# Expert stage of a two-layer diffusion backbone: six fixed split buffers, wider up matmuls, another order of the loads at the start

## The reference, cut to what matters

```
h = x * (1 + sc) + sh;   x = layer_norm(alpha * x + gate * f(h))     # each of four sub-layers
sh, sc, gate, ... = split(silu(c) @ w_mod + b_mod)                   # the modulation
hc = ctx * (1 + csc1) + csh1;   k_c, v_c = hc @ w_kv                 # context keys and values, layer 0
# experts: rows of x sorted by expert
top_logit, top_e = top_k(h @ w_router, 2);  gates = softmax(top_logit)
for e in range(8):                                                   # D = 1024, hidden 3584
    y[rows of e] = (silu(h[rows] @ w1[e]) * (h[rows] @ w3[e])) @ w2[e]
out = sum over a token's two experts of gate * y
```

## Time and profile before

| | |
|---|---|
| median of 3 runs | 2552.37 us (2550.55 to 2554.25) |
| the profiled execution | 2551.86 us, span 2550.1 us |
| TensorE busy | 2309.6 us, 91% of the span |
| VectorE, ScalarE, GpSimd busy | 1509.1, 1115.8, 346.6 us |
| moved | 514.6 MB, 202 GB/s over the span |

### The profile page before, as it was taken

One profiled execution on the slowest core, in us unless ns is written; L12 is line 12 of the kernel. 1 busy time (PEld: TensorE's weight loads), 2 busy tenths in 40 slices (PEclk: granted clock), 3 DMA queues, 4 the chain that ended last, 5 costly groups with the idle time before them and its releaser, 6 DMA issues.

```text
span 2550.1 us, 38310 instructions
## 1 busy us (share of the span) xinstructions
PE 2309.6 (91%) x14692; PEld 2024.5 (79%) x14693; DVE 1509.1 (59%) x1340; ACT 1115.8 (44%) x1075; POOL 346.6 (14%) x211
## 2 busy tenths in 40 slices
PE   5999979999987996698999999999999999999990
PEld 4866757887875875588999999988888889998880
DVE  3456565434476445487444444468888884445886
ACT  3135432222223223476333433357777774334771
POOL 0000118888560000100000000000000000000004
PEclk7989989999998996799999999999999999999995
DMA  6420155554431211788544545468898885545873
GB/s 279 182 83 1 71 230 194 183 183 149 179 116 66 99 66 50 268 335 303 187 180 174 200 180 183 181 243 329 335 346 325 345 334 209 190 171 197 313 279 132
DMA packets 76452, 514.62 MB, mean 202 GB/s; under 512 B 8272, under 2 KB 8400, under 8 KB 19056
## 3 DMA queue, kind: packets, MB, share of 16 engines
q1 hardware_dynamic: 61632, 444.55, 46.7%
q0 software_dynamic: 14768, 69.35, 7.4%
HBM read 484.51 MB, written 29.36 MB: 202 GB/s over the span
## 4 chain that ended last, share of the span: by engine, by line
PE 82%; DVE 10%; issue 3%; ACT 2%; DMA 2%; POOL 0%; DVEq 0%; ACTq 0%; SPq 0%; POOLq 0%
PE ps L1427 25%; PE ps L1429 24%; PE ps L1428 24%; DVE lo L1001 3%; PE ps L540 2%; PE ps L495 2%; PE ps L551 2%; PE ps L1665 1%; DVE hl L1352 1%; DMA raw<-w_mod 1%; PE ps L499 1%; PE ps L1468 1%; DMA xg<-dispatched_x 0%; DVE xz L1097 0%; DVE rstd L1091 0%
## 5 line engine op out<-in xcount | busy, mean ns | idle before, releaser
L1001 DVE TENSOR_TENSOR lo<-raw,hi 128x2048 fp32r<-128x2048 f32 x397 | 928.4, 2357 | 214.4 <-ACT hi L767 212.1
L767 ACT ACTIVATE hi<-raw 128x2048 fp32r<-128x2048 f32 x397 | 760.0, 1914 | 507.2 <-PE ps L1429 497.9
L1427 PE MATMUL ps<-hi,xth 128*128 128x256 f32 x2464 | 706.1, 287 | 13.8 <-DVE xtl L1332 12.9
L1429 PE MATMUL ps<-hi,xtl 128*128 128x256 f32 x2464 | 700.0, 284 | 0.0
L1428 PE MATMUL ps<-lo,xth 128*128 128x256 f32 x2464 | 699.9, 284 | 0.0
L1427 PEld LDWEIGHTS ps<-hi,xth 128*128 128x128 f32 x2464 | 475.3, 193 | 25.3 <-DVE xtl L1332 14.3
L1428 PEld LDWEIGHTS ps<-lo,xth 128*128 128x128 f32 x2464 | 475.5, 193 | 1.9
L1429 PEld LDWEIGHTS ps<-hi,xtl 128*128 128x128 f32 x2464 | 475.3, 193 | 0.0
L1427 PE MATMUL ps<-ah,hi 128*128 128x512 f32 x688 | 272.4, 396 | 19.2 <-DVE al L1063 12.9
L1427 PE MATMUL ps<-hi,hh 128*128 128x512 f32 x616 | 248.8, 404 | 28.9 <-DVE hl L1352 28.9
L1428 PE MATMUL ps<-al,hi 128*128 128x512 f32 x688 | 270.7, 393 | 0.0
(11 more groups left out here) (230 smaller groups left out, 2490.7 us busy)
## 6 DMA issues: line engine op xcount, KB each, us to landing
raw<-w_moe SPq DMA_DIRECT2D x338, 1024.0 KB, 4.8
raw<-w_pre SPq DMA_DIRECT2D x59, 1024.0 KB, 4.8
raw<-w_mod POOLq DMA_DIRECT2D x28, 1024.0 KB, 5.1
raw<-w_mod SPq DMA_DIRECT2D x20, 1024.0 KB, 7.2
dispatched_x<-zt POOLq DMA_DIRECT2D x22, 512.0 KB, 15.0
xg<-dispatched_x POOLq DMA_DIRECT2D x8, 1024.0 KB, 5.8
expert_y<-ys POOLq DMA_DIRECT2D x8, 1024.0 KB, 5.6
expert_y<-zt POOLq DMA_DIRECT2D x6, 512.0 KB, 24.6
```

What stands on the lines that cost most here:

```text
L767: act.activation(HI[h][:], RAW[r][:], ACT.Copy).then_inc(hi_ready[h], 1)
L1001: dve.tensor_tensor(LO[h][:], RAW[r][:], HI[h][:].bitcast(F32), ALU.subtract).then_inc(raw_used[r], 1)
L1427: pe.matmul(outp, wh, ah, start=first, stop=False, skip_group_check=True)
L1429: return pe.matmul(outp, wl, ah, start=False, stop=last, skip_group_check=True)
```

## The change

In the expert stage: six pairs of split buffers in place of three. Units 0 and 1 lie side by side in one tile (`HIA`, `LOA`), 2 and 3 in another, so that one up matmul takes 2x256 columns, w1 and w3 of one half, into one bank per row tile. The order in an expert is staggered over the halves and groups; the down product of the second half runs in the next group, behind up of the first half. The next expert's rows are transposed in the last group, ahead of its last down product. ScalarE and VectorE no longer wait for TensorE at each position, but at the silu and at the transposed hidden tile, whose waits cover the buffers. The result is started by `start` flags and no longer zeroed. SP's queue waits for the first rows to land before it loads on. The overflow path is rewritten alike.

At the start: another order of the loads; the first split is made while modulation is still running; the small matmuls run between the units of w_mod; ScalarE makes the high parts of context and x from the source; TensorE takes the context tile by tile.

```diff
+        HIA = put("hia", [P, 2, KD, 256], F32R, o_hi)      # LOA at o_lo, HIB at o_ah, LOB at o_al
+        HI5 = put("hi5", [P, UNIT], F32R, r2 + 49152)
+        LO5 = put("lo5", [P, UNIT], F32R, r2 + 57344)
-        MOE_BODY = [(p, p % 3) for p in range(6)]
+        WHERE = {0: (0, 0), 1: (1, 1), 5: (2, 5), 2: (3, 3), 3: (4, 4), 4: (5, 2)}   # unit: raw, split
 SP, start
-            for u in range(MOD_A):
+            for u in range(6):
                 load(u % 4, w_mod[u])
-            sp.dma_start(MASKF[:], maskin[:, 1, :]).then_inc(mask_in, 16)
             sp.dma_start(CX[:], ctxT_in).then_inc(cxin, 16)
             load(0, w_pre[0])
+            for u in (6, 7):
+                load(u % 4, w_mod[u])
             sp.dma_start(XZ[:], xT_in).then_inc(xin, 16)
+            sp.dma_start(MASKF[:], maskin[:, 1, :]).then_inc(mask_in, 16)
 SP, experts
+            def next_units(at):
+                for j in (0, 1):
+                    load(WHERE[j][0], unit(at + (6 + j)))
+                load(WHERE[5][0], unit(at + 5))
+                for j in (2, 3, 4):
+                    load(WHERE[j][0], unit(at + (6 + j)))
+            first_units(0, (0, 1, 2))
+            sp.wait_ge(stats_in, 3)
+            first_units(0, (3, 4))
             sp.wait_ge(routed, 1)
-            sp.wait_ge(scattered, 16 * 8)
+            sp.wait_ge(xg_in, 16)
+            with t.loop(sp, NE * GROUPS - 1, RAW_TURN) as g:
+                next_units(g * 6)
 ScalarE, start
+            for p in range(3):
+                mod_row(p)
+            full_split(0, 0)
+            mod_row(3)
...
             for k in range(KD):
-                act.wait_ge(ctx_tmp, k + 1)
-                act.activation(CXH[:, k, :], TMP[k % 2][:, 0:CTX], ACT.Copy).then_inc(cxh_ready, 1)
+                act.activation(CXH[:, k, :], CX[:, k, :], ACT.Identity, bias=MOD[:, 1, k:k + 1],
+                               scale=CG[:, k:k + 1]).then_inc(cxh_ready, 1)
+            act.wait_ge(xin, 16)
             for k in range(KD):
-                to_hi(k)
+                act.activation(AH[:, k, :], XZ[:, k, :], ACT.Identity, bias=MOD[:, 0, k:k + 1],
+                               scale=COEF[:, 0, 0, k:k + 1]).then_inc(ah_ready, 1)
+            act.wait_ge(tmp_ready, KD)
             for k in range(KD):
                 act.activation(XZ[:, k, :], XZ[:, k, :], ACT.Copy, scale=ALPHA).then_inc(alpha_done, 1)
 ScalarE, experts
+            def silu(q):
+                act.wait_ge(up_done[q], t.n(("up", q)))
+                act.activation(SE[:], up_view(q, 0), ACT.Silu).then_inc(se_ready, 1)
+            def group(upto=None):
+                silu(0)
+                high(0)
+                hidden(0)
+                high(1)
+                high(5)
+                silu(1)
+                high(2)
+                hidden(1)
+                if upto is not None:
+                    for i in range(3):
+                        token_tiles(i)
+                high(3)
+                if upto is not None:
+                    token_tiles(3)
+                    result(upto)
+                high(4)
 VectorE, start
+            split(0, 0)                      # now ahead of the modulation's sums
-            for k in range(KD):
+            for k in range(KD + 1):          # TMP of tile k, then CXL of tile k - 1
 VectorE, experts: group()
+                gated(0)
+                low_part(4)
+                hidden(0)
+                low_part(0)
+                low_part(1)
+                gated(1)
+                low_part(5)
+                hidden(1)                    # last group: token_tiles(0..2)
+                low_part(2)                  # last group: token_tiles(3), result
+                low_part(3)
 TensorE, start
-            for u in range(MOD_A):
-                mod_unit(u % 4, PS[:, u // 2, (u % 2) * 256:(u % 2 + 1) * 256])
+            for p in range(MOD_A // 2 + 1):  # two units, then the four small matmuls of the pair before
...
-            pe.wait_ge(cxl_ready, KD)
-                            for c in range(2):
-                                for k in range(KD):
+                            for k in range(KD):
+                                pe.wait_ge(cxl_ready, k + 1)
+                                for c in range(2):
 TensorE, experts
+            def up(q, tiles, r=None):
+                for j in (2 * q, 2 * q + 1):
+                    arrived(j)
+                hi, lo = ((HIA, LOA), (HIB, LOB))[q]
+                for s in range(tiles):
+                    for i, k in enumerate(ks):
+                        ins = three(PS[:, 2 * q + s, :], XTH[:, k, cols_], XTL[:, k, cols_],
+                                    hi[:, :, k, :], lo[:, :, k, :], i == 0, i == KD - 1)
+                ins.then_inc(up_done[q], 1)
+            def expert(tiles, r, more):
+                up(0, tiles, r)
+                turn_hidden(0, tiles)
+                up(1, tiles)
+                pe.wait_ge(ys_a, r)
+                pe.wait_ge(ys_b, r)
+                down(0, tiles, True)
+                turn_hidden(1, tiles)
+                with t.loop(pe, GROUPS - 1, turn):
+                    up(0, tiles)
+                    down(1, tiles)
+                    turn_hidden(0, tiles)
+                    up(1, tiles)
+                    down(0, tiles)
+                    turn_hidden(1, tiles)
+                if more:
+                    pe.wait_ge(xg_in, r * 16 + 16)
+                    for i in range(3):
+                        token_tiles(i)
+                down(1, tiles).then_inc(y_full, 1)
+                if more:
+                    token_tiles(3)
```

More of the change, by code:

```diff
@@ L262, in program @@
         raw_used = [sem(f"raw_used{i}") for i in range(6)]
[L263 removed]
+        hi_ready = [sem(f"hi_ready{i}") for i in range(6)]
         unit_done = [sem(f"unit_done{i}") for i in range(3)]
@@ L626, in _ @@
             t.skip(("raw", 3), 1)
-            per_g = {("raw", r): 1 for r, _ in MOE_BODY}
             def unit(i):
                 return w_moe[bass.ds(i, 1), :, :].rearrange("o p n -> (o p) n") if not isinstance(i, int) else w_moe[i]
-            def group(first):
-                for j in range(2, 8):
-                    load(j % 6, unit(first + j))
-            for j in range(4):
-                load(j, unit(j))
-            sp.wait_ge(routed, 1)
-            sp.wait_ge(scattered, 16 * 8)
@@ L643, in _, with first_units @@
-            for j in range(4, 8):
-                load(j % 6, unit(j))
-            with t.loop(sp, GROUPS - 1, per_g, 1) as g:
-                group(g * 6)
-            with t.loop(sp, NE - 1, times(per_g, GROUPS), 1) as e:
-                with t.loop(sp, GROUPS, per_g) as g:
-                    group(e * (6 * GROUPS) + g * 6)
+            def first_units(at, units):
+                for j in units:
+                    load(WHERE[j][0], unit(at + j))
+            def next_units(at):
[4 more added lines that the diff above has]
+                    load(WHERE[j][0], unit(at + (6 + j)))
@@ L653, in _ @@
[L653 to L655 removed]
+                with t.loop(sp, n_over, times(RAW_TURN, GROUPS)) as x:
                     e = sp.value_load(RI[0:1, bass.ds(x + 8, 1)], min_val=0, max_val=NE - 1)
[L657 to L660 removed]
+                    first_units(e * (6 * GROUPS), (0, 1, 2, 3, 4))
+                    with t.loop(sp, GROUPS - 1, RAW_TURN) as g:
+                        next_units(e * (6 * GROUPS) + g * 6)
+                    load(WHERE[5][0], unit(e * (6 * GROUPS) + (6 * GROUPS - 1)))
@@ new lines, in last_group @@
+            def last_group(r):
+                silu(0)
+                hidden(0)
+                high(5)
+                silu(1)
+                hidden(1)
+                result(r)
+            turn = dict(RAW_TURN)
+            turn.update({("up", 0): 1, ("up", 1): 1, "ht": 2})
+            turn_e = times(turn, GROUPS)
+            turn_e["xt"] = 4
+            for j in (2, 3, 4):
+                high(j)
+            for i in range(4):
+                token_tiles(i)
+            with t.loop(act, NE - 1, turn_e) as e:
+                with t.loop(act, GROUPS - 1, turn):
+                    group()
+                group(e + 1)
@@ new lines, in last_group @@
+            def last_group(r):
+                gated(0)
+                low_part(4)
+                hidden(0)
+                gated(1)
+                low_part(5)
+                hidden(1)
+                result(r)
+            turn = {("hs", h): 1 for _, h in WHERE.values()}
+            turn.update({"se": 2, "hh": 2})
+            turn_e = times(turn, GROUPS)
+            turn_e["xth"] = 4
+            dve.sem_inc(ys_b, 1)
+            dve.wait_ge(scattered, 16 * 8)
+            low_part(2)
@@ new lines, in either @@
+            def either(e, r, more):
+                count = pe.value_load(RI[0:1, bass.ds(e, 1)], min_val=0, max_val=T)
+                saved = dict(t.at)
+                with pe.If(count < P + 1):
+                    expert(1, r, more)
```

(8 more changed lines are left out.)

372 lines of the change are left out of this document (170 added, 202 removed).

## The result

The changed kernel takes 2439.37 us (median of 4 runs, 2438.57 to 2440.11); the kernel before, run beside it, 2552.11 (4 runs, 2550.55 to 2554.25). The ratio is 0.9558, with a 95% interval of 0.9541 to 0.9574: 113 us faster. The forecast was 2454, 15 us above, inside the range. The profiled execution took 2438.57 us, 0.8 under the median (span 2436.7).

The account below looks back on a forecast made before the run. TensorE was taken as the bound, four fifths of the chain of waits, mostly one split matmul's three partial products. Terms 23 + 54 + 3.5 + 6.4 + 10.5 = 97.4; 2551.9 - 97.4 = 2454 us; 8-in-10 range 2434 to 2488.

Parts of the forecast that it names:

- two-tile groups: Groups of 512 hidden features in experts over 128 rows: wider up matmuls give 33.75 us, 1.11 less; 21 groups, 23 us.
- one-tile groups: Groups in experts whose rows fit one tile: TensorE alone sets 17.3 us against 18.83; 35 groups, 54 us gained.
- between experts: Row transposes, splits and hand-overs between the eight experts: 42.3 us falls to 38.8, 3.5 us gained.
- start of the experts: First load of an expert's rows no longer shares with weight loads: lands in 5.8 us, not 12.2; 6.4 us gained.
- start of the kernel: Earlier context and first-unit loads and splits: second weight unit ready at 58.7 us against 69.47, 10.5 us gained.
- (d): Up matmuls: widening is worth nothing, 512 columns cost 0.240 us; 2495 us; chance 0.04.
- The layout of the group: One-tile group: down covers silu and product, VectorE is never behind, every wait is covered; 17.3 us.
- (a): One-tile groups: DMA sets the pace, about 18 us a group; 24 less gained, 2478 us; chance 0.12.
- (b): One-tile groups: hand-overs decide, a split ahead of a small op stalls each half; 18.3 us, 2490 us; chance 0.12.
- (c): Up matmuls: the two-piece moving operand restarts the stream, 0.31 us apart; slower, about 2756 us; chance 0.03.
- the gap rule: Up matmuls: columns divided by the clock plus some 2.5 ns, so a merged pair saves only 2.5 ns; sum 2486.
- The 358 GB/s: One-tile groups' weight loads: HBM side binds a core near this rate; 17.6 us a group, sum 2464.

Follow-up runs that it names:

- narrow: The changed kernel with each up matmul of 512 columns cut back into two of 256; order, buffers and waits stay: 2483.14 us.
- less_pe: The changed kernel without the third partial product (high weights by the hidden tile's low part) of every down projection: 2323.29 us.
- less_pe_half: The changed kernel without the down projections' third partial product and without half the columns of each load of an expert's next weight unit: 2322.96 us.
- contig: The changed kernel with a half's two units interleaved in the split buffers, so the up matmuls' moving operand is one run of 512 columns: 2439.57 us.
- fill: The changed kernel with the transposes of an expert's first hidden half moved behind the first twelve matmuls of its second up half: 2430.69 us.
- no_cover: The changed kernel with the down product of the half before put ahead of up 0; buffers, width and other engines' order stay: 2606.98 us.
- start_only: The kernel before with only the edits of the start of the kernel, the experts untouched: 2542.69 us.
- fill_early: fill with the high part of the second weight unit made ahead of the scaling of x on ScalarE: 2430.47 us.
- fill_first: fill with, on VectorE in an expert's first group, the second half's product put ahead of the low part of next unit 1: 2440.3 us.

## Why the prediction was right, and where its sizes were off

The direction and the place of each gain were right. Within the span, before and after differ by 113.4 us, and the traces divide them so:

| step | forecast | measured | from |
|---|---|---|---|
| two-tile groups, 21 | 23 | 26.3 | 34.86 - 33.61 |
| one-tile groups, 35 | 54 | 68.6 | 18.83 - 16.87 |
| between experts | 3.5 | 3.0 | rest 42.3, now 1335.6 - 1296.3 = 39.3 |
| start of the experts | 6.4 | 6.9 | rows' issue to first up, 15.5 and 8.6 |
| start of the kernel | 10.5 | 10.7 | first scatter 1027.97 and 1017.28 |
| end of the kernel | 0 | -2.0 | last store to end, 59.3 and 61.3 |

**The mis-sized term is the one-tile group: 17.3 forecast, 16.87 measured, 14.6 us over 35 groups, nearly all that the forecast was high; the other differences add up to 1.5.** Two things were wrong in "72x0.229 + 0.84". First the pace: the eleven intervals of the earlier trace rows that gave 0.229 begin with the first matmuls of a run, which are the slow ones. In after the matmuls of 512 columns stand 0.2267 us apart, up and down alike, read from the starts of two runs of down matmuls: 1693.98 to 1696.47 is 11 intervals of 0.2266, 1702.41 to 1704.00 is 7 of 0.2267. That makes 72 x 0.0023 = 0.17 us a group. The two starts of the first run in after:

```profile
1693.98 0.39 PE L1509 MATMUL ps<-hi,hh 128*128 128x512 f32 x1
...
1696.47 0.39 PE L1511 MATMUL ps<-hi,hl 128*128 128x512 f32 x1
```

Second, the 0.84 that I took over as "transposes and restarts" was the remainder behind one named stall. In after the remainder is 16.87 - 72 x 0.2267 = 0.55, so 0.29 of it was something else. The trace of before has it: a second wait for VectorE, once in a one-tile group, behind the transposes. The transposes and the next weight load in before:

```profile
1743.12 0.38 PE L1665 MATMUL ps<-small,he 128*128 128x128 f32 x2
...
1743.52 0.19 PEld L1427 LDWEIGHTS ps<-hi,xth 128*128 128x128 f32 x1 [0.26 <-DVE lo L1001]
```

And its waits in 1700 to 1837 us, the seven groups of one expert:

```profile
PEld ps L1427 <- DVE lo L1001: 1.8, 7, 0.3
```

From these transposes to the next matmul 0.40 us pass in 33 of the 35 one-tile groups; behind the group's other transposes it is 0.13, and in after and narrow it is 0.13 behind both, an expert's first and last group aside. So 0.27 us a group were a wait for the low part of unit 3, which the prediction did not name, and 0.27 + 0.17 is the 0.43 by which the term was off. (What the expectation of narrow calls a restart of 0.27 was this wait: narrow's own is 0.13.)

In the two-tile group, where TensorE never waited for VectorE, the remainder did carry over: 33.61 - 144 x 0.2267 = 0.97, and before, with the same pace for its 48 down matmuls, 34.86 - 23.04 - 10.88 = 0.94. (My 33.75 was also slightly off its own terms: 144 x 0.229 + 0.85 is 33.8.) That difference between the two kinds of group is the mark of a stall inside a remainder.

**Between the experts the sum came out near by luck.** In after a one-tile expert lasts 121.8 us, 3.7 more than its seven groups, where 1.9 + 0.5 + 0.3 + 2.05 = 4.75 was laid out. Seven times 1.0 less is balanced by what the layout had not: the idle of 4.70 us and the lower clock behind it, 2.6 us.

narrow shows how the one-tile term divides: the forecast 54 was 18 for the width (the 18 that rival (d) takes away) and 36 for order and buffers; measured are 20 and 49. The width was right, and the whole miss lies in order and buffers.

**The layout of the group held.** Down covers silu and product; VectorE is on time in each half, with 0.40 us to spare where I had laid out 0.3 (14.7 to 15.0). The one place that I named as uncovered, an expert's first group, shows 1.79 us against 2.05.

**The start.** The first context matmul is at 37.69 where I said 35.6. TensorE in after, the modulation matmuls before it:

```profile
27.90 1.94 PE L1550 MATMUL ps<-raw,silp 128*32 128x256 f32 x16 [4.72 <-DMA raw<-w_mod]
30.38 1.94 PE L1550 MATMUL ps<-raw,silp 128*32 128x256 f32 x16 [0.54 <-DMA raw<-w_mod]
32.24 3.58 PE L1566 MATMUL ps<-sel,mp 128*128 128x2 f32 x16
37.69 0.55 PE L1509 MATMUL ps<-cxh,hi 128*128 128x256 f32 x1 [1.88 <-DVE cxl L1092]
```

I had four small matmuls left behind the last unit (1.75 us); there are eight, which the trace counts as sixteen (3.58 us), and they make 1.8 of the 2.1 us. It cost less than that: the second unit starts at 59.73 (forecast 58.7) and decides, as forecast, because ScalarE makes its high part behind the scaling of x, 4.28 us from 50.81.

**Rivals.** (a) did not happen. The DMA share did rise to 0.97 and landing to 7.0 us, exactly the signs that I would have read as a limit; less_pe and less_pe_half show that it was none. (b) is refuted by VectorE's rows above, (c) by contig, (d) by narrow. That a split ahead of a small operation can hold TensorE up is seen in fill, once in each one-tile expert. In no_cover the hand-overs themselves are bare, and no split stands ahead of them.

**The rules that were weighed.** Matmuls of 512 columns 0.2267 us apart and pairs of 256 at 2 x 0.120 = 0.240: the gap rule of "TensorE: Matmul & The Clock Gate", section "Back-to-back issue gap", in the Trainium skill would have had the pair 2.5 ns dearer than the merged matmul; here it is 13 ns, which is what made the widening worth 44 us. That section gives the rule for an isolated matmul, and for a stream of weight loads and matmuls some 131 ns at 512 columns. This kernel is such a stream, at 226.7 ns, so neither figure fits it. The 358 GB/s of "DMA: Bandwidth & Descriptors", section "Where 436 GB/s comes from", in the Trainium skill is passed by 385 over 126 us in after and 415 over 60 us in less_pe: with one core at work it bounds nothing here. The same section mentions a measurement of 425 GB/s as well, which none of these passes.

**What stays open.** The end of the kernel is 2.0 us longer in after: the first gather of results starts 7.81 us after GpSimd's last store by an idle that no row explains (5.70 before). start_only, with the old experts, has 58.9 us there, so the 2 us come with the change of the experts; no run isolates them further. Open too are the idle of 4.70 us at the first two-tile expert, which before has as well, and why the clock falls behind some waits and not behind others.

**The best version** is fill, or fill_early, which measures the same: 2430.7 and 2430.5 us, 0.953 and 0.952 of the kernel before, some 8 us under the changed kernel.

## What to carry to other kernels

When a producer chain (silu, product, transpose, copy, subtract) stands between two matmul stages, give TensorE a block of independent matmuls longer than that chain, and lay out in time what each helper engine does in between; six buffers without that order were slower here than three (2606.98 us). When a period is forecast from the old one, name what is in the remainder before carrying it over: a remainder next to a stall is partly stall. A DMA share near 1.00 is no proof of a limit; halve the bytes and see whether the time moves.

## What the hardware showed that was not expected

- **The DMA share does not measure load.** 366 GB/s showed 0.97, 415 GB/s showed 1.00, and with loads of half the length 216 GB/s still showed 0.66. The share counts the time that packets are under way, and that time stretches: landing went from 4.8 to 7.0 us between before and after without any engine waiting for it.
- **Kernels whose start is the same start differently.** The second weight unit starts at 59.73 and 59.70 us in the two runs of after, but at 57.70 in no_cover, 58.15 in narrow, 59.59 in fill and 60.92 in less_pe, whose code up to there is the same; the first scatter lies between 1015.11 (fill) and 1020.87 (less_pe_half). So some 3 us either way belong to the program as a whole and not to an edit. The cause was not looked for. It bounds what a total time can say: the start of the kernel gained 9.7 or 10.7 us in this trace, with that much uncertainty, and effects under 5 us were read here from the stretch between first up matmul and last store. That stretch is not free of chance either: the lower clock at the first two-tile expert costs 2.6 us in after and 1.2 in fill.
- **The granted clock fell behind some waits of TensorE and not behind others.** In fill_first five waits of 1.76 us are alike; behind three of them the clock is at its lower level for about 3 us, behind two it is not. Behind the 4.70 us idle it was lower in every profiled run of the new experts. So a wait of 1.76 us cost up to 1.6 us more than its own length, or nothing more.
- **A moving operand in two pieces of 256 columns 8 KB apart streams like one run of 512**: 2439.57 against 2438.89 us over 3696 such matmuls.
